# Relative-bias rows: two products and two repeated writes in place of twelve, and the first stage's modulation parts moved earlier

## The reference

```python
def t5_bucket(dist): ...                       # 32 buckets of the distance
s_w = einsum(q, k) * scale + head_bias[:, :, t5_bucket(dist_w)]   # 8 heads, window 512
s   = einsum(q, k) * scale + head_bias[:, :, t5_bucket(dist)]     # 4 heads, window 128

c_act, cc_act = silu(c), silu(c_ctx)           # c: (1, 1024)
mod_l = c_act  @ ada_w[i] + ada_b[i]           # ada_w: (2, 1024, 6 * 1024)
mod_c = cc_act @ ada_w[i] + ada_b[i]
```

## Time and profile before

| | us |
|---|---|
| Median of 3 runs | 2524.95 |
| Lowest and highest | 2523.92, 2529.55 |
| The profiled execution | 2529.77 |
| Its span in the trace | 2528.0 |
| TensorE busy in it | 2478.3 |
| VectorE busy | 1616.3 |
| ScalarE busy | 1191.9 |
| GpSimd busy | 336.6 |
| DMA, bytes | 401.65 MB, mean 159 GB/s |

### The profile page before, as it was taken

The page is one execution under the profiler, slowest core; times in us unless marked ns, Lnnn a source line. Parts: engine busy times, 40 slices in busy tenths (PEclk is TensorE's granted clock), DMA queues, the critical chain, the costliest instruction groups (busy, mean ns, idle before and its releaser), DMA issues.

```text
span 2528.0 us, 42325 instructions
## 1 busy us (share of the span) xinstructions
PE 2478.3 (98%) x18041; PEld 2312.9 (91%) x18041; DVE 1616.3 (64%) x2444; ACT 1191.9 (47%) x1960; POOL 336.6 (13%) x375
## 2 busy tenths in 40 slices
PE   8999999999999999999999999999999999999998
PEld 7999989999999999899999667888889999999998
DVE  4787566788888865767775875542433654456753
ACT  5444465544444455655554553531333534345643
POOL 1321000332022110032341000100001011001000
PEclk8999989999999999999999999999999999999999
DMA  7667544576777766447785120332332433334552
GB/s 241 206 224 205 156 150 132 163 245 225 254 239 240 238 148 190 117 148 269 267 269 156 52 68 19 99 100 84 100 100 84 128 107 110 100 101 153 173 192 100
DMA packets 386385, 401.65 MB, mean 159 GB/s; under 512 B 44695, under 2 KB 370611, under 8 KB 385940
## 3 DMA queue, kind: packets, MB, share of 16 engines
q1 hardware_dynamic: 383448, 391.19, 49.6%
q10 hardware_dynamic: 2748, 7.76, 0.9%
HBM read 394.72 MB, written 4.19 MB: 158 GB/s over the span
## 4 chain that ended last, share of the span: by engine, by line
PE 79%; DVE 12%; ACT 4%; issue 2%; DMA 2%; POOL 1%; SPq 0%; DVEq 0%; ACTq 0%; POOLq 0%
PE bank L676 23%; PE bank L677 23%; PE bank L678 23%; DVE rounded L2424 6%; PE bank L684 4%; ACT rounded L1642 2%; DVE plain L2409 2%; PE bank L1565 2%; PE bank L689 2%; DMA plain<-in_w_in 1%; POOL plain L3507 1%; PE bank L1090 1%; DMA plain<-in_ffn_w_gate 1%; PE bank L1120 1%; PE bank L779 0%
## 5 line engine op out<-in xcount | busy, mean ns | idle before, releaser
L676 PE MATMUL bank<-rounded 128*128 128x256 f32 (+1 forms) x3704 | 1119.9, 302 | 8.6 <-DVE rounded L2424 4.5
L677 PE MATMUL bank<-rounded 128*128 128x256 f32 (+1 forms) x3704 | 1103.2, 298 | 0.0
L678 PE MATMUL bank<-rounded 128*128 128x256 f32 (+1 forms) x3704 | 1102.7, 298 | 0.0
L2424 DVE TENSOR_TENSOR rounded<-plain,rounded 128x1024 fp32r<-128x1024 f32 (+1 forms) x630 | 741.8, 1224 | 464.6 <-ACT rounded L1642 464.3
L1642 ACT ACTIVATE rounded<-plain 128x1024 fp32r<-128x1024 f32 (+1 forms) x630 | 616.3, 1032 | 306.3 <-PE bank L678 194.8
L676 PEld LDWEIGHTS bank<-rounded 128*128 128x128 f32 x3704 | 717.8, 194 | 43.1 <-issue 9.2
L677 PEld LDWEIGHTS bank<-rounded 128*128 128x128 f32 x3704 | 718.2, 194 | 16.2
L678 PEld LDWEIGHTS bank<-rounded 128*128 128x128 f32 x3704 | 717.5, 194 | 16.4
L676 PE MATMUL bank<-rounded,rounded 128*128 128x256 f32 (+2 forms) x1472 | 450.9, 306 | 8.7 <-DVE plain L2625 3.2
L678 PE MATMUL bank<-rounded,rounded 128*128 128x256 f32 (+2 forms) x1472 | 448.5, 305 | 0.0
L677 PE MATMUL bank<-rounded,rounded 128*128 128x256 f32 (+2 forms) x1472 | 447.5, 304 | 0.0
(11 more groups left out here) (310 smaller groups left out, 2004.9 us busy)
## 6 DMA issues: line engine op xcount, KB each, us to landing
plain<-in_mlp_w SPq DMA_DIRECT2D x64, 1024.0 KB, 5.3
plain<-in_ada_w SPq DMA_DIRECT2D x48, 1024.0 KB, 5.6
plain<-in_ffn_w_gate SPq DMA_DIRECT2D x44, 1024.0 KB, 5.4
plain<-in_ffn_w_up SPq DMA_DIRECT2D x44, 1024.0 KB, 6.2
plain<-in_ffn_w_down SPq DMA_DIRECT2D x32, 1024.0 KB, 5.4
plain<-in_w_in SPq DMA_DIRECT2D x32, 1024.0 KB, 5.5
plain<-in_od_w_in SPq DMA_DIRECT2D x32, 1024.0 KB, 5.7
plain<-in_ffn_w_down SPq DMA_DIRECT2D x16, 768.0 KB, 5.6
```

The costliest lines, as they stand in the source:

```text
L676: pe.matmul(dst, a[0], b[0], start=first and i == 0, stop=False)
L677: pe.matmul(dst, a[0], b[1], start=False, stop=False)
L678: ins = pe.matmul(dst, a[1], b[0], start=False, stop=last and i == n - 1)
L2424: dve.tensor_tensor(low, raw, top, SUB).then_inc(*done(("lo", m, half)))
```

## The change

The twelve products become two. `REL` names the groups of heads (0 to 8, 8 to 12). In step 1 the product of group 0 has 8 columns of `rel_bias` as weights and gives a bank with one row for each head (8 partitions by 512); in step 2 that of group 1 gives 4 partitions by 512. Step 3 has none. ScalarE copies 8 (or 4) partitions and issues one DMA, whose source repeats each partition's 2 KB 128 times; the destination is the same as before, 2 MB for the first group and 1 MB for the second. Bytes written are the same, read from partitions 0 to 7 and 0 to 3 instead of from all 128. The wait of the first `ada` unit remains, now for product 1 and for the second write.

In `ADA`, the eight units `ada` of stage `a0` are placed after steps 7, 9, 11, 13, 15, 17, 19 and 23 instead of 7, 11, 15, 19, 22, 24, 26 and 28. The two chunks that they fill are thus transposed and reduced at steps 13 and 14 and steps 23 and 24, instead of 19 and 20, and 28 and 29.

```diff
-ADA = {"a0": [7, 11, 15, 19, 22, 24, 26, 28], ...
+ADA = {"a0": [7, 9, 11, 13, 15, 17, 19, 23], ...
+REL = [(0, 8), (8, 12)]
 # TensorE, prepare
-            for h in range(4 * step - 4, 4 * step):
-                b = bank("rel", h)
-                half = 0 if h < 8 else 512
+            if step < 3:
+                g = step - 1
+                b, (h0, h1) = bank("rel", g), REL[g]
...
-                pe.matmul(b[:, :], M.relx[0:33, h:h + 1].to_broadcast([33, 128]), M.onehot[0:33, half:half + 512],
-                          start=True, stop=True).then_inc(*done(("rel", h)))
+                pe.matmul(b[0:h1 - h0, :], M.relx[0:33, h0:h1], M.onehot[0:33, 512 * g:512 * g + 512],
+                          start=True, stop=True).then_inc(*done(("rel", g)))
 # ScalarE, prepare
-            for h in range(4 * step - 4, 4 * step):
-                b = M.bank("rel", h)
-                for s in new(at("rel", h), at("flat", h - 4) if h >= 4 else None):
+            if step < 3:
+                g = step - 1
+                h0, h1 = REL[g]
+                row = M.rrow[g][0:h1 - h0, :]
+                for s in new(at("rel", g)):
                     act.wait_ge(*s)
-                act.activation(M.rrow[h % 4], b[:, :], ACT.Copy, scale=1.0).then_inc(...)
+                act.activation(row, M.bank("rel", g)[0:h1 - h0, :], ACT.Copy, scale=1.0).then_inc(...)
...
-                act.dma_start(M.flat[h, :].rearrange("(p n) -> p n", n=512), M.rrow[h % 4]).then_inc(...)
+                act.dma_start(M.flat[h0:h1, :].rearrange("h (p n) -> h p n", n=512),
+                              row.unsqueeze(1).broadcast_to([h1 - h0, 128, 512])).then_inc(...)
 # VectorE, summed, first ada unit
-            for s in new(at("cc"), at("cols", 1), at("cols", 2), at("rel", 11), *[at("flat", h) for h in range(8, 12)]):
+            for s in new(at("cc"), at("cols", 1), at("cols", 2), at("rel", 1), *[at("flat", h) for h in range(8, 12)]):
```

More of the change, by code:

```diff
@@ L93 @@
 CHUNKS = ([(0, ch, (0, 1)) for ch in range(6)] + [(1, ch, (0, 1)) for ch in range(2)] + [(1, ch, (0,)) for ch in range(2, 6)])
-ADA = {"a0": [7, 11, 15, 19, 22, 24, 26, 28], "b0": [1, 4, 6, 9, 12, 14, 17, 19, 23, 26, 28, 31],
+ADA = {"a0": [7, 9, 11, 13, 15, 17, 19, 23], "b0": [1, 4, 6, 9, 12, 14, 17, 19, 23, 26, 28, 31],
        "a1": [1, 4, 6, 9, 12, 14, 17, 19, 23, 25, 27, 30],
@@ L1748, in prepare @@
         elif step < 4:
-            for h in range(4 * step - 4, 4 * step):
-                b = M.bank("rel", h)
-                for s in new(at("rel", h), at("flat", h - 4) if h >= 4 else None):
+            if step < 3:
[3 more added lines that the diff above has]
+                for s in new(at("rel", g)):
                     act.wait_ge(*s)
-                act.activation(M.rrow[h % 4], b[:, :], ACT.Copy, scale=1.0).then_inc(*done(("rrow", h), ("free", "rel", h)))
-                for s in new(at("rrow", h)):
+                act.activation(row, M.bank("rel", g)[0:h1 - h0, :], ACT.Copy, scale=1.0).then_inc(
+                    *done(("rrow", g), ("free", "rel", g)))
+                for s in new(at("rrow", g)):
                     act.wait_ge(*s)
-                act.dma_start(M.flat[h, :].rearrange("(p n) -> p n", n=512), M.rrow[h % 4]).then_inc(
-                    *M.land(f"flat{h % 4}").done(("flat", h)))
+                act.dma_start(M.flat[h0:h1, :].rearrange("h (p n) -> h p n", n=512),
+                              row.unsqueeze(1).broadcast_to([h1 - h0, 128, 512])).then_inc(
+                    *M.land(f"flat{g}").done(*[("flat", h) for h in range(h0, h1)]))
     def context(step):
```

## The result

| | before | after |
|---|---|---|
| Median, us (range, runs) | 2527.25 (2523.92 to 2531.58, 4) | 2589.6 (2580.98 to 2592.08, 4) |
| Span of the profiled execution | 2528.0 | 2586.5 |

The change makes the kernel slower, by 62 us: ratio 1.0235, interval 1.0206 to 1.0263. The forecast was 2570, its range 2506 to 2600.

The account below looks back on a forecast made before the run. TensorE, busy 98% of the span, was taken as the bound. Waiting for the second write makes it resume 42.9 us later, plus 2.0 for the clock, 0 for modulations: +44.9 on 2525.0 gives 2570, range 2506 to 2600.

Parts of the forecast that it names:

- The products: Stage `a0`, TensorE: ten of twelve bias products go and the clock stays up, gaining 15.5 us, at least 11.5.
- The writes: Bias-row writes from 8 and 4 partitions take 78 us side by side; the second lands at 114.9.
- Rival 3: Both writes take turns, as both read partitions 0 to 3: 132 us, landing 165.3, time 2620; chance 0.12.
- The landing at 110: Second write's landing by the skill's port rule: 2.1 MB through the first port, 77 us; time 4 us shorter.
- Who waits: VectorE stands at the first `ada` unit from 53.3 to 114.9; TensorE goes on at 122.5, 42.9 us later.
- even if they are slowed by the writes they have 50 us: Block 4's weight loads on SyncE's queue have 50 us during the wait; their slowing was costed at nothing.
- the sign: If TensorE waits longer than VectorE, the writes starved the loads, a cause costed at nothing.
- The prediction's single cause: TensorE loses time because VectorE waits for the second write to land; starved loads were costed at nothing.
- The modulations: Denser `ada` units in stage `a0`: VectorE's debt and the relieved stage end balance; 0 taken, bounds -4.6 and +8.
- The debt of VectorE: VectorE's 12.3 us against TensorE's 11.5 per block: 0.8 in six blocks, 2.9 for each reduction, up to 8 us.
- three units of lead: The lead in stage `a0` that should bear most of VectorE's debt of up to 8 us.
- the relieved end: End of stage `a0`: TensorE idle times of 1.42, 1.56 and 1.63 us, behind reductions that move away.

Follow-up runs that it names:

- the version with 128 partitions: Changed kernel with old modulation places and head columns repeated in the weights, so both writes read all 128 partitions: 2516.92 against 2530.22 us, ratio 0.9944.
- the late-modulation pair: First-stage modulation units at 15, 17, to 29, with the changed kernel's writes and with the old ones: ratios 1.0174 and 1.0018 against the kernel before.
- the writes alone: Changed kernel with the first stage's modulation units at their old places: 2584.04 against 2530.22 us for the kernel before, ratio 1.0239.

## Why the prediction was right, and where its size was off

- **The products.** Right. 15.5 us worked out, 15.25 found in the version with 128 partitions. A new product took 1.02 us for its two matmuls, as priced, and the clock did not fall. In the changed kernel the gain is spent in the wait, as forecast.
- **The writes.** Right in kind, landing at 122.08 against 114.9 forecast, but that it came so near is luck. The forecast had two writes side by side, each at a rate counted by partitions (3 to 4 GB/s each) and so 78 us long. The runs show another law: four neighbouring partitions give the writes 24 to 25 GB/s together, and the number of engines is the outermost count. Both writes read partitions 0 to 3 through the same first four engines, and these packets can only follow one another, 128 for each engine and write: 256 at 0.34 us are 87 us, from 33.7 to 121. A rate per partition that was too low and a term for taking turns that was left out nearly made up for one another. Rival 3 had the turns, with 66 us for a write where it is 43.
- **The Trainium skill's rule** (SBUF — State Buffer, "Door 1: The DMA port swizzle") is borne out in its grouping: partitions 0 to 3 are one way and 0, 4, 8, 12 are four, which no count of partitions would give. Its figure of about 27 GB/s for each way is near the 24 to 25 measured here for the writes. The landing at 110 that the prediction worked out from it was 12 us early. The division among engines, stated in DMA: Bandwidth & Descriptors, "Why a DMA increments its semaphore by 16 and not by 1", is what the DMA shares of 0.26 and 0.51 show.
- **Who waits.** TensorE goes on at 128.21, where 122.5 was forecast. The chain landing, additions, low parts is as told: 122.08 + 3.9 + 2.3. But TensorE stood for 46.11 us then and not 58, and VectorE came to the unit at 75.3 and not at 53.3, as both had been held up before.
- **What was wrong: "even if they are slowed by the writes they have 50 us".** The loads were slowed enough to stop TensorE on their own: the 9.57 us before 74.02, when VectorE wasn't waiting for the landing yet, and the weights rounded at 98.50. The prediction had named the sign, TensorE idle for longer than VectorE waits; it is 58.9 against 46.8 us. In the changed kernel it costs little more, as both waits run beside one another; but the late-modulation pair shows 39 us of cost without any wait for the landing, of the 51 to 60 that the writes cost in all. The prediction's single cause was one of two, each nearly enough.
- **Not foreseen:** ScalarE held 13 us by the issue. It makes the first stop, 3.19 us; its cost by itself wasn't tried.
- **The modulations** were the mis-sized term: 0 taken, with bounds of -4.6 and +8. Alone they cost 0.43%, 11 us (6 to 16), and 6.7 at the stage's end. The debt of VectorE was rightly named, but its terms add up to 10.6 and not 8 (six times 0.8 and twice 2.9). That three units of lead would bear most of it, and that the relieved end would pay it back, was wrong.
- **A slip in the range:** with a write of 66 us and -4.6 for the modulations the sum gives 2553, where 2549 stands.

By the stage ends: 44.9 forecast and 5.7 for the later restart (the landing 7.2 later, the additions 1.3 shorter) are 50.6, against 51.0 for the writes alone; the places add 7.1, and together it is the 58.1 measured there. The 62 us of the whole kernel have an interval of 52 to 66, and the 4 us that are left lie within it.

## What to carry to other kernels

A DMA that repeats few rows saves compute and costs transfer: before writing it, count over how many groups of partitions its source is spread, and what its outermost dimension counts. Repeating the rows in the product (a matmul of it takes 0.59 us with 8 columns of weights, and 0.59 to 0.69 with 128) and again in the DMA gave both the two-instruction product and the full rate. And a slow DMA has to be priced twice: by who waits for it, and by who shares its engines. When a rate is read from a row of the profile, ask whose bytes are in it: here a third were loads.

## What the runs showed of the hardware

- Writes out of SBUF in 2 KB packets, loads not counted: neighbouring partitions 0 to 3 on 4 engines 24 GB/s, 0 to 7 on 8 engines 48, 0 to 15 on 16 engines 98. Partitions 0, 4, 8, 12 on 4 engines, beside loads: 66. A packet took 0.30 us in the first and 0.085 us in the last.
- Two queues on one engine took turns packet for packet (354 of the writes to 355 of the loads in 30 us), so that 0.30 us for each packet of the writes slowed the loads' 1 KB packets to one each 0.34 us, and 1 MB over 16 engines to 22 us.
- Two writes of together 1536 pieces of 2 KB, 256 of them on each of the first four engines, held the issuing queue for 12.99 to 13.53 us; with the faster source 2.38 us, and with the pieces on 16 engines 0.55 and 0.58. With the slow writes under way and the modulations late, issues of loads on SyncE's queue were held too, for 9.59 to 13.61 us.
- Three groups of products of 3.6 to 4.1 us each, with 33 rows of weights, brought the granted clock to 0.50 while TensorE was never idle; single products of 1.0 us did not, with 8 and 4 columns of weights or with 128.
